# The end of a two-block transformer kernel: how the final norm is summed, weighted, applied and stored

## The reference

```python
def rmsnorm_2(x, g):
    xf = x.astype(jnp.float32)
    y = xf * lax.rsqrt(jnp.mean(xf * xf, axis=-1, keepdims=True) + EPS)
    return (y * g.astype(jnp.float32)).astype(x.dtype)

    for l in range(DEPTH):
        ...
        x = x + conv_ffn(x, ffn_norm_g[l], w_gate[l], w_up[l], ffn_conv_w[l], ffn_conv_b[l], w_down[l])
    return rmsnorm_2(x, final_norm_g)
```

## Time and profile before

| | |
|---|---|
| median of 3 timed runs | 2491.25 us (2489.78, 2491.25, 2499.22) |
| profiled execution | 2489.32 us |
| its span | 2488.0 us, 37723 instructions |
| mean granted clock of PE | 0.989 of 2.4 GHz |
| busy: PE, PEld, DVE, ACT, POOL | 97%, 87%, 67%, 45%, 11% |
| DMA | 428 MB, mean 172 GB/s |

### The profile page before, as it was taken

How to read it: one execution, slowest core, us unless ns; L and a number is a source line. 1 busy time by engine, 2 the same in 40 slices (tenths; PEclk the granted TensorE clock), 3 DMA queues, 4 the chain that set the end, 5 groups by cost and what they waited for, 6 DMA issues and landing times.

```text
span 2488.0 us, 37723 instructions
## 1 busy us (share of the span) xinstructions
PE 2418.3 (97%) x15414; PEld 2153.4 (87%) x15414; DVE 1663.4 (67%) x2304; ACT 1118.3 (45%) x1481; POOL 261.4 (11%) x129
## 2 busy tenths in 40 slices
PE   8999999999999999999899999998999999999997
PEld 7888699888888888889897898897888888888886
DVE  5998756666666666677676443366776766767677
ACT  4000445544544454454536345555444444444443
POOL 0000000000000000004333433330010100000000
PEclk9999999999999999999899999999999999999998
DMA  7445466666666666655434355453666666566663
GB/s 233 153 144 171 159 195 193 190 192 188 192 188 187 195 187 189 193 152 154 117 107 126 106 149 150 158 187 119 193 188 191 189 190 192 188 192 188 187 194 119
DMA packets 379628, 428.11 MB, mean 172 GB/s; under 512 B 16409, under 2 KB 328001, under 8 KB 379457
## 3 DMA queue, kind: packets, MB, share of 16 engines
q1 hardware_dynamic: 374336, 421.58, 55.1%
q10 hardware_dynamic: 5120, 4.12, 0.5%
HBM read 423.54 MB, written 3.67 MB: 172 GB/s over the span
## 4 chain that ended last, share of the span: by engine, by line
PE 91%; DVE 4%; ACT 3%; issue 1%; DMA 0%; POOL 0%; ACTq 0%; DVEq 0%
PE product L563 38%; PE product L565 19%; PE product L512 18%; PE product L537 10%; PE product L534 1%; ACT w_hi L464 1%; DVE w_lo L471 1%; DVE delta_work L1831 0%; DVE heads L2263 0%; DVE x_residual L620 0%; PE small L1594 0%; DVE delta_work L1829 0%; PE small L908 0%; PE small L1608 0%; PE small L1647 0%
## 5 line engine op out<-in xcount | busy, mean ns | idle before, releaser
L471 DVE TENSOR_TENSOR w_lo<-w_raw,w_hi 128x1024 fp32r<-128x1024 f32 x640 | 795.5, 1245 | 516.7 <-ACT w_hi L464 515.7
L464 ACT ACTIVATE w_hi<-w_raw 128x1024 fp32r<-128x1024 f32 x712 | 750.3, 1057 | 834.4 <-PE product L565 578.2
L563 PE MATMUL product<-h_operand,w_hi 128*128 128x512 f32 x2496 | 870.2, 394 | 7.3 <-DVE x_residual L766 7.3
L565 PE MATMUL product<-h_operand,w_lo 128*128 128x256 f32 x2496 | 696.0, 279 | 0.0
L563 PEld LDWEIGHTS product<-h_operand,w_hi 128*128 128x128 f32 x2496 | 468.8, 188 | 114.3 <-DVE x_residual L766 7.8
L565 PEld LDWEIGHTS product<-h_operand,w_lo 128*128 128x128 f32 x2496 | 471.2, 189 | 0.1
L563 PE MATMUL product<-mlp_hidden,w_hi 128*128 128x512 f32 x1024 | 355.7, 394 | 0.9 <-DVE x_residual L620 0.8
L479 POOL TENSOR_TENSOR w_lo<-w_raw,w_hi 128x1024 fp32r<-128x1024 f32 x72 | 182.1, 2530 | 1422.8 <-ACT w_hi L464 1422.8
L565 PE MATMUL product<-mlp_hidden,w_lo 128*128 128x256 f32 x1024 | 283.7, 277 | 0.0
L512 PE MATMUL product<-h_operand,w_hi 128*128 128x256 f32 x1280 | 242.4, 291 | 5.0 <-POOL w_lo L479 3.3
L563 PE MATMUL product<-mid_operand,w_hi 128*128 128x512 f32 x704 | 244.3, 390 | 0.0
(11 more groups left out here) (296 smaller groups left out, 2487.7 us busy)
## 6 DMA issues: line engine op xcount, KB each, us to landing
w_raw<-in_mlp_w SPq DMA_DIRECT2D x256, 512.0 KB, 3.7
w_raw<-in_w_in SPq DMA_DIRECT2D x112, 512.0 KB, 3.8
w_raw<-in_w_gate SPq DMA_DIRECT2D x88, 512.0 KB, 3.6
w_raw<-in_w_up SPq DMA_DIRECT2D x88, 512.0 KB, 4.4
w_raw<-in_w_down SPq DMA_DIRECT2D x88, 512.0 KB, 3.5
w_raw<-in_cc_w_in SPq DMA_DIRECT2D x128, 256.0 KB, 2.9
w_raw<-in_cc_w_out SPq DMA_DIRECT2D x32, 512.0 KB, 4.9
w_raw<-in_w_out SPq DMA_DIRECT2D x32, 512.0 KB, 4.2
```

The costliest lines, as they stand in the source:

```text
L464: act.activation(k.w_hi[i % SPLIT], k.w_raw[i % RAW], ACT.Copy).then_inc(*k.act_done.mark("w_hi", i))
L471: dve.tensor_tensor(k.w_lo[i % SPLIT], k.w_raw[i % RAW], k.w_hi[i % SPLIT].bitcast(F32), ALU.subtract).then_inc(*k.dve_done.mark("w_lo", i))
L563: pe.matmul(out, hi[:, kk, n], x.both[:, kt].rearrange("p a t -> p (a t)"), start=s == 0 and kk == 0, stop=False, skip_group_check=True)
L565: done = pe.matmul(out[:, 0:T], lo[:, kk, n], x.hi[:, kt, :], start=False, stop=last and kk == WIDE_K - 1, skip_group_check=True)
```

## The change

- ACT: squares of group 3 are taken by halves, tiles 12 and 13 as soon as they are added, then 14 and 15. After the squares of each group (or half) it multiplies these tiles of x by the norm's weights in place, one activation per tile (`gained`). In the first step of the last down product it takes the square root of one spare column, whose result is not used.
- DVE: groups 0 to 2 are summed as before; the first halving, 1024 to 512 columns, is done right after group 2. After the last residual addition the squares of tiles 12 and 13 are added and the sum is halved to 256 columns. The squares of tiles 14 and 15 are not added by DVE.
- PE: the total is three products with ones into one bank: the sum, then the squares of tiles 14 and of 15.
- DVE: the row is applied by eight multiplications of a pair of tiles, without the weights.
- SP: eight stores of a pair (256 KB) in place of four of a group.
- One buffer more, a column `spare_column` ahead of most other buffers.

```diff
@@ buffers
         self.row = {norm: rows[:, i % 2, :] for i, norm in enumerate(NORMS)}
+        self.spare_column = self.sbuf("spare_column", [P, 1])
         self.double_gain = self.sbuf("double_gain", [P, KT])
@@ pe_ffn
-    pe_total(k, pe, "final2")
+    bank, free = k.bank.take("total", "final2")
+    for f in free:
+        pe.wait_ge(*f)
+    pe.wait_ge(*k.dve_done.at("sums", "final2"))
+    pe.matmul(bank[:, 0:T], k.m("ones"), k.square_sum[0][:, 0:T], start=True, stop=False, skip_group_check=True)
+    pe.wait_ge(*k.act_done.at("squares", "final2", CT - 1, 1))
+    for t in range(PT):
+        done = pe.matmul(bank[:, 0:T], k.m("ones"), k.sq.at("final2", CT - 1)[:, PT + t, :], start=False, stop=t == PT - 1,
+                         skip_group_check=True)
+    done.then_inc(*k.pe_done.mark("total", "final2"))
@@ act_ffn
+    def gained(b, tiles):
+        act.wait_ge(*k.act_done.last())
+        for n in tiles:
+            done = act.activation(k.x[:, n, :], k.x[:, n, :], ACT.Copy, scale=k.col("final_norm_g_2", n))
+        done.then_inc(*k.act_done.mark("gained", b, tiles[-1] // PT))
+
+    def last_squares(p, half):
+        if half:
+            sq = k.sq.at("final2", CT - 1)
+        else:
+            sq, free = k.sq.take("final2", CT - 1)
+            for f in free:
+                act.wait_ge(*f)
+        tiles = tiles_of(CT - 1, half)
+        act.wait_ge(*k.dve_done.at("added", "ffn_down", p, CT - 1, half))
+        act.activation(sq[:, half * PT:(half + 1) * PT, :], k.x[:, tiles[0]:tiles[-1] + 1, :], ACT.Square).then_inc(
+            *k.act_done.mark("squares", "final2", CT - 1, half))
+        gained(CT - 1, tiles)
+        yield
+
+    def squares_and_gain(p, b):
+        act_squares(k, act, "final2", b, k.x[:, b * CT:(b + 1) * CT, :], k.dve_done.at("added", "ffn_down", p, b))
+        yield
+        for half in range(2):
+            gained(b, tiles_of(b, half))
+        yield
+
     def over(p, b, half):
-        if half:
-            act_next(k, act, "final2", b, None, None, ("ffn_down", p, b))
+        if b == CT - 1:
+            k.act_beside.start(after(1, last_squares(p, half)))
+        elif half:
+            k.act_beside.start(after(1, squares_and_gain(p, b)))
+        if b == 0 and half == 0:
+            act.activation(k.spare_column, k.eps[:, 0:1], ACT.Sqrt).then_inc(*k.act_done.mark())
@@ dve_ffn
-        if p == last and half:
-            k.dve_beside.start(after(1, dve_squares_of_x(k, dve, "final2", b)))
+        if p == last and b < CT - 1 and half:
+            k.dve_beside.start(after(1, sum_squares(b)))
+        if p == last and b == CT - 1 and not half:
+            k.dve_beside.start(after(1, sum_last()))
+
+    out = k.square_sum[0]
+
+    def sum_squares(b):
+        dve_squares(k, dve, "final2", b)
+        if b == CT - 2:
+            dve.wait_ge(*k.dve_done.last())
+            dve.tensor_tensor(out[:, 0:2 * T], out[:, 0:2 * T], out[:, 2 * T:4 * T], ALU.add).then_inc(*k.dve_done.mark("halves added"))
+        yield
+
+    def sum_last():
+        half = k.sq.at("final2", CT - 1)[:, 0:PT, :].rearrange("p k t -> p (k t)")
+        dve.wait_ge(*k.act_done.at("squares", "final2", CT - 1, 0))
+        dve.wait_ge(*k.dve_done.at("halves added"))
+        dve.tensor_tensor(out[:, 0:2 * T], out[:, 0:2 * T], half, ALU.add).then_inc(*k.dve_done.mark())
+        dve.wait_ge(*k.dve_done.last())
+        dve.tensor_tensor(out[:, 0:T], out[:, 0:T], out[:, T:2 * T], ALU.add).then_inc(*k.dve_done.mark("sums", "final2"))
+        yield
...
     dve_row(k, dve, "final2")
-    for g in range(CT):
-        xg = k.x[:, g * CT:(g + 1) * CT, :]
-        dve.wait_ge(*k.act_done.at("squares", "final2", g))
-        dve_norm_group(k, dve, "final2", xg, "final_norm_g_2", g, xg)
+    dve.wait_ge(*k.dve_done.at("row", "final2"))
+    for n in range(KT // PT):
+        pair = k.x[:, n * PT:(n + 1) * PT, :]
+        dve.wait_ge(*k.act_done.at("gained", n // PT, n))
+        dve.tensor_tensor(pair, pair, spread_row(k.row["final2"], PT), ALU.mult).then_inc(*k.dve_done.mark("final", n))
@@ sp_store
-    for g in range(CT):
-        tiles = slice(g * CT, (g + 1) * CT)
-        sp.wait_ge(*k.dve_done.at("group", "final2", g))
-        sp.dma_start(k.dram["out"][tiles].rearrange("k p t -> p k t"), k.x[:, tiles, :]).then_inc(*k.x_stored.mark(g))
-    sp.wait_ge(*k.x_stored.at(CT - 1))
+    for n in range(KT // PT):
+        tiles = slice(n * PT, (n + 1) * PT)
+        sp.wait_ge(*k.dve_done.at("final", n))
+        sp.dma_start(k.dram["out"][tiles].rearrange("k p t -> p k t"), k.x[:, tiles, :]).then_inc(*k.x_stored.mark(n))
+    sp.wait_ge(*k.x_stored.at(KT // PT - 1))
```

## The result

The changed kernel takes 2497.54 us (median of 20 runs, 2495.81 to 2502.72) against 2491.55 us for the kernel before (20 runs). The ratio is 1.0023, with a 95% interval from 1.0016 to 1.0029: the change makes the kernel 6 us slower, 0.2% of its time. The profiled execution took 2498.54 us, its span is 2497.1, 9.1 us more than before. The forecast was 2488.1 and a range that ended at 2497.0.

What follows compares the result with a forecast made beforehand. The prediction took the 18.2 us tail, a chain of engines waiting on each other, as all that could change. Gains of 0.96 + 1.2 = 2.2 us gave 2487.1 from the profile, 2489.05 from the median; forecast their middle, 2488.1, range 2485.2 to 2497.0.

Steps and rivals of the forecast that it cites:

- Nothing but the tail can change.: Whole kernel: the diff sits behind the last matmul of the last product, so only the 18.2 us tail can move.
- The last sign of the prediction: Body of the kernel: the prediction is wrong if the time of the middle of the kernel moves.
- Rival D, the layout: Buffers behind the spare column move; 1 ns on each of 15,414 matmuls makes 15 us longer; chance 0.06.
- The sums, (a) to (e): Tail ahead of PE's total: table load, gains, early halving, split squares, shorter sum; sums ready at 2472.77 instead of 2474.85.
- All covers: Tail: table load and gains fit into ACT's idle time between steps of 2.77 us, at cost 0.
- PE's total: Tail: six passes instead of two, 0.6 us at full clock, ending at 2475.23, bounds 2475.7 and 2474.39.
- The stores: End of tail: eight stores bound by the queue at 351 GB/s, ending T0 + 8.22 against T0 + 9.41, gain 1.2.
- T0: Tail: the start of the scalings, 2478.59 before, forecast at 2477.63, 0.96 earlier (0.5 to 1.8).
- Rival B: Stores: smaller ones flow at 290 GB/s, the 1.2 is gone, gain 0.5, time 2489.8; chance 0.11.
- rival C: Stores: SP can't issue as fast; at 1.89 apart it loses 5.8 us, 2496; chance 0.06.
- the fixed cost without overlap: Stores: 2.0 us fixed per DMA, eight 20.8 us against four 12.8, losing some 7 us; chance 0.01.
- The tail's gain of 2.2: Tail: 0.96 from an earlier T0 plus 1.2 from the stores, from 1.1 to 3.0 us.

Runs made afterwards that it cites:

- e1: The change without the spare column, its square root written into an unused column of the epsilons: 2490.71 us, ratio to the kernel before 1.0002.
- e12: The changed kernel with all three moving operands 32 bytes above a multiple of 128, the weights at a multiple of 128: 2491.30 us, ratio to before 0.9987.
- e13: The kernel before in the layout of e12, its spare column allocated and unused: 2492.15 us, ratio to before 0.9993.
- e15: The change without the spare column, h_operand and mlp_hidden each moved 32 bytes further, all else kept modulo 128: 2490.78 us, ratio to before 0.9988.
- e16: As e15, but with mlp_hidden alone moved and h_operand left where it was: 2489.97 us, ratio to before 0.9995.
- e7: The kernel before with the spare column allocated, all buffers behind it 32 bytes further except mid_operand, which stays: 2493.89 us, ratio to before 1.0013.
- e8: The changed kernel with h_operand, mlp_hidden and mid_operand at odd multiples of 32 bytes, the weights at a multiple of 64: 2507.97 us, ratio to before 1.0059.
- e11: The change without the spare column, with four stores of 512 KB in place of eight of 256 KB: single run, span ending at 2490.18.
- e17: The change as it is with the spare column widened to 128 bytes: 2505.90 us, ratio to before 1.0066.
- e2: The kernel before with the spare column alone allocated, unused: 2500.01 us, ratio to before 1.0030.
- e6: The kernel before with 32 bytes put behind the heads buffers, moving mid_operand, delta_work and the mixer's small buffers: 2498.28 us, ratio to before 1.0036.
- e10: The kernel before with the spare column and with w_hi and w_lo moved by 32 bytes to an odd multiple: 2512.91 us, ratio to before 1.0082.
- e14: e12 with the squares of the last two tiles added by DVE and one product with ones on PE: single run, 7.45 us from PE's last product to T0.

## Why the prediction was wrong

- *"Nothing but the tail can change."* This is the step that failed. I read "the whole diff sits behind the last matmul" as a bound, though one line of the diff is an allocation. The body lost 12.1 us between the two profiles, 8.1 of it in slower steps of PE; by medians the column alone costs 9.1 us (2500.01 against 2490.92). The last sign of the prediction, "if the time of the middle of the kernel moves", is what came.
- *Rival D, the layout*, was the right one: priced by a guess of 1 ns per matmul at 15 us and given 0.06. The size of the price is luck: it put 1 ns on every matmul, 0.016 us on a step, where 146 of the 258 steps of the feed-forward network lost 0.053, 16 lost 0.018 and the others nothing. The chance was too low, and the range, which ended at 2497.0, left out D's own 2505. "No row shows such a thing or excludes it" was true of the rows shown there. But the kernel before had three of its twenty runs at 2499.2 to 2499.5 beside the rest at 2489.8 to 2493.2, and I took the one of them that I saw for scatter. A slow MLP, as in the profile of e1 (248 steps x 0.053 = 13 us), would make such a run; that those three were of this kind was not profiled. Timed beside the experiments, the kernel before had 14 of 86 runs above 2495, and four kernels with `mlp_hidden` at 32 (e12, e13, e15, e16) none of 46, the highest 2494.65. But e7, at the same three distances as e16, had four of twelve above 2495, and the slow steps of its profile were with `h_operand`.
- *The sums, (a) to (e).* Behind PE's last product, forecast and measured: last addition from 0.47 to 1.88 (0.40 to 1.80), last squares done at 2.60 (2.47), sums at 2.96 (2.86), PE's total from 3.11 (3.01). ACT's four gains took 1.85 (1.8), its squares of group 2 came when the addition allowed, and the table load and its root ended 0.25 us before the next copy. All covers held.
- *PE's total.* Forecast 2.31 with 0.6 us at full clock, bounds 1.47 and 2.91; the changed kernel had 1.54, e8 1.86, e1 2.72, e12 2.90. The granted clock in the row below shows the lucky case. The spread of 1.4 was right, and it is a draw, not a gain. The draw mostly falls the other way: of the eight profiles with six passes, six took 2.59 to 2.90, so 0.6 us at full clock was too much.
- *The stores.* Forecast 8.22 behind T0, measured 8.29 in the changed kernel and 8.28 in e12; issues 0.60 apart, a landing in 2.8 us, and 341 GB/s where 351 was taken. Rival B, with 290 GB/s, falls, and so does rival C, that SP can't issue as fast, and with it the fixed cost without overlap, of which the Trainium skill ("DMA: Bandwidth & Descriptors", section "Anatomy of one DMA") would have made 20.8 us for eight stores, an estimate. The section gives that cost for DMAs issued by POOL, which the prediction did not say, and these stores are issued by SP; for them the trace disagrees, since eight issues and all their data took 7.6 us, 2489.49 to 2497.1.

Busy times by window of the changed kernel; the third number from the end is the clock, the last the flow:

```profile
2484.90:2486.40 1.50, 1.50 (x6) 1.03 (x6) 0.00 (x0) 0.40 (x1) 0.00 (x0) 1.00 0.00 0
...
2490.50:2496.50 6.00, 0.00 (x0) 0.00 (x0) 3.17 (x6) 0.00 (x0) 0.00 (x0) 0.50 1.02 341
```

The tail's gain of 2.2 was thus 3.0 in that execution and 1.6 to 2.7 in the six other profiles with eight stores and six passes, mostly by the clock of PE's total. How much of it reaches the time can be read from one pair in the same layout: e12 and e13 differ by 0.85 us in their medians and 1.6 in the tails of their profiles (16.6 and 18.2). With twelve runs each, which scatter by 3 and 4.5 us, the 0.85 is barely clear of the scatter.

Open: why PE is slower at some distances, since no view shows what it waits for inside a matmul; what picks the pace at distance 0; whether `w_lo`, which lies 16384 behind `w_hi` in every kernel, counts by itself; distance 192, which no kernel had; and the length of the mixer, from the MLP's last matmul to the total of the norm ahead of the feed-forward network: 645.8 to 646.4 us in before, e1, e7, e11 and e17, 648.2 to 650.8 in after, e2, e6 and e12 to e16, 650.3 to 652.2 in e8 to e10. Three profiles in one layout (e12, e13, e14) span 2.5 us of it.

## What to carry to other kernels

An allocation is an edit to every buffer behind it. When a change adds or resizes one, print the addresses of before and after, and put new small buffers at the end, or where they move nothing. And if a kernel's times fall into two groups, compare the pace of one repeated step in a run of each before any of the scatter is called noise.

## What the runs showed of the hardware

- PE's pace in a stream of fp32r products changes with the distance in bytes between the moving operand and other buffers, as it seems the weights: between 2.773 and 2.827 us for 16 weight loads and 16 matmuls, 2% of the time, with nothing waited for and the granted clock at 1.00. Over this kernel 64 bytes of gap decide between 2491.3 (e12) and 2508.0 us (e8).
- At some distances the pace is held over hundreds of steps and changes only where products follow one another or stall, so that one program has two times: nine runs of e1 at 2488.6 to 2491.4 us, three at 2497.8 to 2501.9.
- PE resumed at the full clock after 3.01 us of idling in the changed kernel and kept it for six passes; in e12, after 3.07 us, the granted clock was 0.50 from its first pass on and the six took 2.90 us against 1.54.
- Eight stores of 256 KB flow as fast as four of 512 KB: 341 GB/s over 6 us in the changed kernel, 340 over 4.5 us in e11.
